# Attention: in the last group the exponentials of a unit stand ahead of the copy of the unit in front of it on ScalarE

## The reference

```python
q = (xn @ w_q).reshape(bsz, seq, N_DIL_GROUPS, DIL_HEADS, DIL_HEAD_DIM)
for gi, (window, dilation) in enumerate(DIL_PATTERNS):   # (128,1), (512,4), (2048,16)
    o, lse = dilated_window_group(q[:, :, gi], k_sh[:, :, gi], v_sh[:, :, gi], window, dilation)
...
# inside a group: s = q k^T * scale, masked
    m = jnp.max(s, axis=-1, keepdims=True)
    p = jnp.exp(s - m)
    l = jnp.sum(p, axis=-1, keepdims=True)
    o = (p / l) @ v
    lse = (m + jnp.log(l))
...
alpha = jax.nn.softmax(jnp.stack(lses, axis=0), axis=0)
o = jnp.sum(alpha[..., None] * jnp.stack(outs, axis=0), axis=0)
out = o.reshape(bsz, seq, ATTN_OUT_WIDTH) @ w_o
```

## Time and profile before

| | |
|---|---|
| Median of 3 runs | 1648.1 us (1641.85 to 1648.45) |
| The profiled execution's own time | 1652.53 us |
| Its span in the trace, first to last instruction | 1650.8 us |
| Busy: PE, PEld, DVE, ACT, POOL | 1409.6, 1085.9, 1015.6, 817.0, 369.9 us |
| Mean granted clock of TensorE | 0.909 of full speed |

### The profile page before, as it was taken

The page is one execution under the profiler, slowest core; times in us unless marked ns, Lnnn a source line. Parts: engine busy times, 40 slices in busy tenths (PEclk is TensorE's granted clock), DMA queues, the critical chain, the costliest instruction groups (busy, mean ns, idle before and its releaser), DMA issues. The chain is left out here.

```text
span 1650.8 us, 29535 instructions
## 1 busy us (share of the span) xinstructions
PE 1409.6 (85%) x11579; PEld 1085.9 (66%) x11579; DVE 1015.6 (62%) x1325; ACT 817.0 (49%) x1206; POOL 369.9 (22%) x417
## 2 busy tenths in 40 slices
PE   4899995777768989999998289999979799999980
PEld 2273782566666467787877167787858778778770
DVE  5325157444564359899987343675444698989963
ACT  3213234244443136888886133444452378888851
POOL 1000005745555001232231310001120113223202
PEclk9697998599999979999999589999987799999995
DMA  5042115003133159999996333121200699999944
GB/s 160 1 153 102 52 51 219 13 10 89 40 95 96 58 211 329 378 383 377 380 385 247 135 102 109 62 76 52 77 26 1 256 349 386 383 378 384 379 187 160
DMA packets 172089, 302.46 MB, mean 183 GB/s; under 512 B 34480, under 2 KB 44848, under 8 KB 171984
## 3 DMA queue, kind: packets, MB, share of 16 engines
q1 hardware_dynamic: 159408, 271.59, 46.1%
q0 software_dynamic: 11520, 25.19, 4.2%
q10 hardware_dynamic: 1056, 4.19, 0.6%
HBM read 279.96 MB, written 35.65 MB: 191 GB/s over the span
## 5 line engine op out<-in xcount | busy, mean ns | idle before, releaser
L1376 DVE TENSOR_TENSOR moe_wlo<-moe_raw,moe_whi 128x2048 fp32r<-128x2048 f32 x160 | 365.7, 2289 | 37.6 <-ACT moe_whi L1372 33.3
L1372 ACT ACTIVATE moe_whi<-moe_raw 128x2048 fp32r<-128x2048 f32 x192 | 366.9, 1917 | 23.6 <-PE all_bank L1385 22.3
L1383 PE MATMUL all_bank<-moe_whi,moe_xhi 128*128 128x512 f32 x512 | 207.7, 406 | 4.2 <-DVE moe_xlo L1432 4.2
L1384 PE MATMUL all_bank<-moe_wlo,moe_xhi 128*128 128x512 f32 x512 | 200.3, 391 | 0.0
L1385 PE MATMUL all_bank<-moe_whi,moe_xlo 128*128 128x512 f32 x512 | 200.2, 391 | 0.0
L1383 PEld LDWEIGHTS all_bank<-moe_whi,moe_xhi 128*128 128x128 f32 x512 | 96.4, 188 | 27.4 <-DVE moe_xlo L1432 4.4
L1385 PEld LDWEIGHTS all_bank<-moe_whi,moe_xlo 128*128 128x128 f32 x512 | 96.4, 188 | 21.2
L1384 PEld LDWEIGHTS all_bank<-moe_wlo,moe_xhi 128*128 128x128 f32 x512 | 96.6, 189 | 18.2
L1383 PE MATMUL all_bank<-moe_whi,moe_hhi 128*128 128x512 f32 x256 | 102.1, 399 | 7.6 <-DVE moe_hlo L1456 7.6
L1548 POOL COPY moe_idxcol<-moe_idx 128x1 int32 (+1 forms) x30 | 33.9, 1130 | 313.5 <-PE all_bank L1395 313.5
L1384 PE MATMUL all_bank<-moe_wlo,moe_hhi 128*128 128x512 f32 x256 | 101.3, 396 | 0.0
(11 more groups left out here) (414 smaller groups left out, 2990.3 us busy)
## 6 DMA issues: line engine op xcount, KB each, us to landing
moe_raw<-in_moe_w_gate_dram SPq DMA_DIRECT2D x64, 1024.0 KB, 9.6
moe_raw<-in_moe_w_up_dram SPq DMA_DIRECT2D x64, 1024.0 KB, 9.6
moe_raw<-in_moe_w_down_dram SPq DMA_DIRECT2D x64, 1024.0 KB, 8.7
attn_xhat<-in_w_kv_dram SPq DMA_DIRECT2D x10, 1024.0 KB, 5.0
out_dram<-all_gain SPq DMA_DIRECT2D x1, 8192.0 KB, 22.3
attn_xhat<-in_attn_w_q_dram SPq DMA_DIRECT2D x6, 1024.0 KB, 5.1
all_h<-in_rwkv_w_v_dram SPq DMA_DIRECT2D x4, 1024.0 KB, 8.3
all_h<-in_rwkv_w_k_dram SPq DMA_DIRECT2D x4, 1024.0 KB, 6.7
```

Of the source, the lines that this page charges most:

```text
L1372: nc.scalar.activation(whi[slot % SPLITS][:, :], raw[slot % 6][:, :], ACT.Copy).then_inc(m["hi_ok"], 1)
L1376: nc.vector.tensor_tensor(wlo[slot % SPLITS][:, :], raw[slot % 6][:, :], whi[slot % SPLITS][:, :].bitcast(fp32), ALU.subtract).then_inc(m[ ...
L1383: nc.tensor.matmul(bank[b][:, :], hi[:, k0 + k, :], wh[:, k, :], start=begin and k == 0, stop=False)
L1384: nc.tensor.matmul(bank[b][:, :], hi[:, k0 + k, :], wl[:, k, :], start=False, stop=False)
```

## The change

For units 24 to 31 ACT issues E(u), F(u), C(u-1) in place of C(u-1), E(u), F(u). Units 1 to 23 and the last copy, C(31), stay as they are, and no other engine's list changes. No semaphore is added.

```diff
             def attend(u):
                 gi, hh, jp = units[u]
-                if u >= 1:
+                if 1 <= u < FAR_AT:
                     transposed(u - 1)
                 act.wait_ge(max_ok, u + 1)
                 if u >= 2:
...
                 if gi > 0:
                     act.wait_ge(d_ok, u - MID + 1)
                     nc.scalar.activation(fold(fade[gi], hh), fold(fade[gi], hh), ACT.Exp).then_inc(e_ok, 1)
+                if u >= FAR_AT:
+                    transposed(u - 1)
```

## The result

The changed kernel takes 1654.16 us (median of 12 runs), the kernel before 1648.28 us (12 runs alongside): 1.0035 times, with a 95% interval of 1.002 to 1.0051. It is slower, by an amount that a single comparison of this kernel just tells from nothing.

The account below looks back on a forecast made before the run. The prediction took an engine-to-engine chain ending at T(31) as the bound; losses of 0.19, 0.59, 0.50, 0.59 and 0.59 summed to 2.46 us, ratio 1.0015, so 1648.1 us became 1650.6 us, range 1644.5 to 1655.5.

Parts of the forecast that it names:

- The chain through ACT, DVE and PE, and T(31) as its end: Last eight units: no engine is full; a chain passes between engines, and any lateness of T(31) delays the kernel.
- Unit 24, 0.19: C(23) ends the group 0.19 us later, with piece 17's split behind it; V(23) stays covered with 0.18 us to spare.
- Units 25, 29 and 31, 0.59 each: PE's transposes now wait for the copy behind E and F: 2.29 us after E instead of 1.70, loss 0.59 each.
- Unit 28, 0.50: The split directly behind F(28) now has C(27) ahead of it: loss 0.50 us, passed on to M(29) and E(29).
- no wait at T(28): Sign expected in the changed kernel's profile: T(28) starts without a wait, with 12 matmuls ahead of it.
- Units 26, 27 and 30, nothing: Exponentials may start up to 0.50 us sooner, costed at nothing; PE's 12 matmuls, 3.29 us, hide the copies.
- The sum, 2.46: At T(31): 0.19 + 0.59 + 0.50 + 0.59 + 0.59 = 2.46 us later.
- The price of a low block, 2.7: T(29) and its 12 matmuls took 6.01 us against 3.29 at T(25): a whole low-clock block costs 2.7 us.
- The clock taken at zero: PE's added falls and give-backs (0.9 us at T(29), 1.2 at T(31)) counted zero; -2.1 and +2.7 kept for the range.
- The forecast's likeliest case: Loss of 2.46 us at T(31) with the clock about as before: 1650.6 us, chance 0.50.
- the first rival: Clock falls at T(25), adding 1.5 to 2.7 us: 1652.1 to 1653.3 us; chance 0.24, shared with a longer low spell.
- The long low spell behind T(31), priced at 8.5 us: Rival: PE's half-speed spell of 19.4 us from T(31) goes away, winning some 8.5 us: 1642 us, chance 0.05.

Follow-up runs that it names:

- The halves of the change: Against the kernel before, copies moved behind the exponentials only at units 25, 28, 29, 31: ratio 1.002; only at units 24, 26, 27, 30: 0.9994.
- the clock held equal: 38 unread 512-column matmuls put into PE's idle times in both kernels: changed kernel 0.9945, kernel before 0.9926 of the kernel before without them.
- early splits: ACT's splits of piece 17 and the first half of the output weights one unit earlier: kernel before 0.9941, changed kernel 0.9957 of the kernel before.
- The half of the change that carries the whole loss: Against the kernel before, only the copies ahead of E(25), E(28), E(29) and E(31) move behind them: ratio 1.002 (1.0008 to 1.0032).

## Why the prediction was right or wrong

- **The chain through ACT, DVE and PE, and T(31) as its end**: right. The halves of the change and the moved splits confirm it; both splits moved by one unit shorten the way by 9 us, 2.5 of it through the clock.
- **Unit 24, 0.19**: right, 0.18, and V(23) kept its cover.
- **Units 25, 29 and 31, 0.59 each**: the mechanism was right, the size 0.08 low each. The step from the copy's end to T was taken as 0.05; in the trace the copy ends at 1206.45 + 0.57 = 1207.02 and T(25) starts at 1207.17, so it is 0.15.
- **Unit 28, 0.50**: right, 0.48. What I passed over is that T(28) waits for C(27) as well, 0.70 us. It cost nothing, since S(30) behind it waits for DVE in any case, 2.29 us. I had said that the 12 matmuls ahead of T(28) hide it, and they don't quite; no wait at T(28) was among the signs that I gave.
- **Units 26, 27 and 30, nothing**: right in this kernel. With early splits it would have been wrong.
- **The sum, 2.46**: 2.67 by the trace's parts, 2.52 with the clock held equal.
- **The price of a low block, 2.7**: the sum compared two different ends, T(29) to DVE's copy (6.01) with T(25) to T(26) (3.29). From T(29) to T(30) it took 5.82, so that block cost 2.53. The block behind T(25) then cost 2.66 in the first trace with the change, but 1.51 in the other three (4.80 against 3.29).
- **The clock taken at zero**: this is the step that failed. The forecast's likeliest case had no fall at T(25), and the first rival had it, with 1.5 to 2.7 us and 1652.1 to 1653.3. The trace has the fall, at 2.66 us, which is more than the whole sum. Of it 1.23 us were given back behind T(29) (I had allowed 0.9); in the other three traces with the fall and the moved copies nothing was given back there, and the fall was the shorter one. Either way some 1.4 to 1.5 us are left against a trace of the kernel before without a fall at T(25). The 1.2 us that I allowed behind T(31) didn't come: +0.46 in this trace, and 0.3 to 0.5 less in the further ones, 45.60 and 45.65 against 46.07 and 45.98. I said that nothing ties the spells to either side; but the rows ahead of the prediction had one fall after a wait of 1.81 us, and the change raises one wait from 1.44 to 2.11, past it. That should have given the rival more than 0.24. With 2.11 us of wait ahead of T(25) the clock fell in four traces of four. The Trainium skill ("TensorE: Matmul & The Clock Gate", "Why this matters for your kernels") advises against idle gaps between bursts of matmuls, but it speaks of longer ones than any wait ahead of T(25). So it doesn't by itself give the low block that the prediction drew from it; the runs show the fall behind a shorter wait.
- **The long low spell behind T(31), priced at 8.5 us**: the size was about right. Where the experiments kept the clock up there, the way from T(31) to the next stage took 36.7 us, 9.2 less than before. The change itself didn't bring that about.
- **The number**: 1654.16 us lies above the likeliest case (1650.6) and above the fall at T(25) (1653.3). It is inside the range through the 2.4 us allowed for the spread of the runs, and that is luck rather than mechanism.
- **What stays open**: the chain's 3.6 us are 0.22%, and the measured ratio is 0.35% with an interval from 0.20 to 0.51. The half of the change that carries the whole loss gave 0.20% (0.08 to 0.32). The rest, some 2 us, is within the intervals, and no trace shows a place for it. Parts of the program that no change touches vary by more than that: V(23) starts at 1198.21, 1193.54 and 1200.84 us in the three traces of the changed kernel.

## What to carry to other kernels

An instruction that an engine runs while it would otherwise wait is free; behind the instruction that it waits for, it costs its length at every place where that one ends last (here 0.67 us for a copy of 0.57). So before two instructions are swapped, look at which of the two was waiting for whom, unit by unit, and look again after each other change to the schedule. Where the chain hands from engine to engine through PE, count also what each longer wait of PE does to its clock; here it cost 1 to 1.5 us on top of 2.5, and holding the clock up through one wait, that ahead of T(31), was worth 9 us, more than the order of all the copies.

## What the runs showed of the hardware

- Small differences in PE's idle time bear on the clock: 1.44 us ahead of T(25) brought a fall in one trace of four, 2.11 us in four of four. Idle time further back seems to count as well: 1.44 us ahead of T(29), with 2.46 us ahead of the scores in front of it, brought a fall in four of four.
- A clock that was high at the start of the far values, a stretch of 64-column matmuls and transposes, stayed high in it, in three kernels of three: 14 matmuls of 512 columns in the wait ahead of T(31) kept it at 1.00 through 13.6 us. Without them PE was just as busy, 19.37 us of 19.40, and the clock stayed at 0.50. The price is 9 us.
- A longer low spell was followed by a shorter one: the three traces of the changed kernel have 5.95, 4.80 and 4.80 us behind T(25) and 4.58, 5.76 and 5.85 us behind T(29), so that the way to T(31) agrees within 0.1 us. It isn't a rule: in the kernel before, the trace with the extra fall (4.86 us) has 6.04 us behind T(29) and gave nothing back. What sets the lengths stays open.
